# The weighted sum of the experts' second rows moves from VectorE to TensorE, in column tiles of 32

## The chip, the core and the metric

The kernel runs on one core of a Trainium2 chip. The metric is device time in microseconds (us) from start to end of one execution. The kernel before was run three times: 2932.58 us in the median (2925.65 to 2934.63).

## The reference, cut to what matters

Two transformer blocks follow each other on 512 tokens of width 1024, all in fp32. The first block has a state-space mixer and then a feed-forward of retrieved experts; the second has attention with pooling and then a gated feed-forward. The change touches the experts. For each token `xb`, 8 heads choose 16 of 16384 experts each, 128 in all. Every expert has a first row `u` and a second row `v` of 1024 numbers:

```
        i1 = jnp.take_along_axis(si[:, :, 0], ci // PEER_TOPK, axis=-1)
        i2 = jnp.take_along_axis(si[:, :, 1], ci % PEER_TOPK, axis=-1)
        eidx = i1 * PEER_N_KEYS + i2
        g = jax.nn.softmax(cs, axis=-1)
        u = expert_u[eidx]
        v = expert_v[eidx]
        act = jax.nn.gelu(jnp.einsum('td,thkd->thk', xb, u).astype(jnp.float32), approximate=False)
        return jnp.einsum('thk,thkd->td', (g * act).astype(v.dtype), v)
```

So 128 dot products with first rows give 128 weights, and the output is the sum of 128 second rows with these weights. The rows are read from memory: 512 tokens x 128 experts x 2 rows of 4 KB.

## The kernel before

The 512 tokens are four tiles of 128, with a token on each partition. The first block's mixer runs for tiles 0 and 1 (mixer 0) and then for tiles 2 and 3 (mixer 1), each followed by the choice of experts ("choose": queries and scores by TensorE, top-k by VectorE, then `slots`, `first` and `index`, which leave the expert numbers in `eidx`). The second block runs as attention of tiles 0 and 1, attention of tile 2, feed-forward of tiles 0 to 2, attention of tile 3, feed-forward of tile 3 (`SECOND`).

Beside this main stream runs the expert stream. Per tile it has 256 steps. In each, GpSimd issues one indirect DMA (L650), which gathers one row for each of the 128 tokens into one of eight buffers (`ring`, 128 x 1024): step k of the first half ("dots") takes the first row of every token's k-th expert, step k of the second half ("rows") takes the second row. VectorE works on each: the dots are multiply-and-sum against the token's own row `u2` (L1827), 128 columns of `dots`. Then ScalarE takes the gelu, VectorE multiplies by `gate` into `wgt`, and in the rows half each gathered tile is multiplied by a column of `wgt` and added to `acc` or `junke` in turn (L1833). `h3` adds the two to the token tile `h2`, and norms it; the second block may start on that tile only then. Gather number i waits until VectorE has done step i - 8, which frees its buffer.

Weights of the main stream come through three slots (`wr`), loaded by SyncE's queue. PSUM has eight banks: two rings of four, "lo" and "hi", from which each product takes the next bank, and waits until that bank's last reader is done.

The order on each engine is fixed when the program is built. `make_plan` merges the two streams by two clocks: the main stream's advances by its planned TensorE time or 1.5 times its planned VectorE time, whichever is more, times a pace for attention; the expert stream's by `EW[t]` (1.5, 1.6, 1.3, 2.0) a step. The stream that is behind goes next. Each engine then walks the same list of units and issues what it has in each, so an engine that waits in one unit holds back all later ones on it.

Of the kernel before, what the change touches and what calls it, by code (L numbers as in the profile page):

```python
# [7 lines left out]
U32 = mybir.dt.uint32  # L8
# [27 lines left out]
EW = (1.5, 1.6, 1.3, 2.0)  # L36
# [58 lines left out]
class Plan:  # L95
# [3 lines left out]
    def __init__(self):  # L99
        self.units, self.bank, self.slot, self.loads = [], {}, {}, []  # L100
        self.turn = {"lo": 0, "hi": 0}
        self.use = [None] * 8
        self.p = self.v = 0.0
# [6 lines left out]
    def take(self, key, which, emptied):  # L110

        i = self.turn[which] % 4 + (4 if which == "hi" else 0)
# [161 lines left out]
def plan_choose(pl, A, q, t0, t1, done):  # L274
# [12 lines left out]
    for hj in range(16):  # L287
# [6 lines left out]
        if hj % 2:  # L294
# [3 lines left out]
            yield True  # L298
    for t in range(t0, t1):
        pl.add("slots", q, t, v=2 * (vc(2048) + 0.2))  # L300
        pl.add("first", q, t, v=3 * vc(2048) + 1.0)
        yield True
        pl.add("index", q, t, v=vc(2048) + 0.4)
# [4 lines left out]
def plan_attend(pl, A, t0, t1):  # L308
# [31 lines left out]
    for u_ in range(len(units) + 2):  # L340
        for lag, part in enumerate(("front", "texp", "mixv")):
            if 0 <= u_ - lag < len(units):
# [5 lines left out]
                elif part == "texp":  # L348
                    while pl.turn["hi"] % 4 < 2:
                        pl.turn["hi"] += 1  # L350
                    pl.take(("texp", t, h), "hi", ("act", "texp", t, h))
                    pl.add("texp", t, h, p=0.12 * (t + 1))
                else:
                    if h == 0:
                        pl.hold(("mixv", t), 4 + t % 2, ("dve", "attn", t))
# [13 lines left out]
def plan_feed(pl, A, t0, t1):  # L369
# [12 lines left out]
    for hf in range(2):  # L382
        bs = list(range(nt)) if hf == 0 else list(range(4, 4 + nt))
        for t in range(nt):
            pl.hold(("down", t0, hf, t), bs[t], ("dve", "down", t0, hf, t))
# [67 lines left out]
def build(nc, A, out):  # L453
    with ExitStack() as ctx:
# [33 lines left out]
        junke = sb("junke", [128, 1024])  # L488
# [74 lines left out]
        with ExitStack() as pk:  # L563
            kT = sbx(pk, "kT", [128, 4, T])
# [46 lines left out]
        jobs = [u[1:] for u in pl.units if u[0] == "expert"]  # L611
        job_of = {u: i for i, u in enumerate(jobs)}
# [28 lines left out]
        def gpsimd(e):  # L641
            w = Waits(e)
            issued, chosen, base = 0, 0, 0

            def gather(k):
                t, which, j = jobs[k]
                w.wait_ge(*dve.at("index", t))
                if k >= NR:
                    w.wait_ge(*dve.at("expert", *jobs[k - NR]))
                e.indirect_dma_start(ring[k % NR][:], None, A[which],  # L650
                                     bass.IndirectOffsetOnAxis(ap=eidx[:, t, j:j + 1], axis=0)
                                     ).then_inc(gathered[k % NR], 16)
# [1303 lines left out]
```

## Time and profile before

| | |
|---|---|
| median of the runs | 2932.58 us |
| the profiled execution | 2928.44 us |
| its span | 2926.6 us |
| mean granted clock of TensorE | 0.826 of full |
| ScalarE busy | 638.5 us (22%) |
| GpSimd busy | 1261.4 us (43%) |
| read from memory | 793.75 MB |

The profile is of one execution, and its span runs from the first to the last instruction. Busy shares are means over stretches with different limits, so a table of stretches is read beside them. In the trace each fp32 matmul of the program is two records. `ring<-in_pu` are the gathers of first rows, `ring<-in_pv` those of second rows. All but a few of TensorE's matmuls go through one helper (L678), so they are told apart by their tiles and shapes.

### The profile page before, as it was taken

To read this page: it belongs to the slowest core of one execution; us is meant where nothing else is said; L and a number is where in the kernel's file an instruction comes from. 1 tells how busy PE (TensorE), PEld (TensorE's weight loads), DVE (VectorE), ACT (ScalarE), POOL (GpSimd) and SP (SyncE) were. 2 spreads that over 40 slices of the span, in tenths; PEclk is the share of its full clock that TensorE was granted. 3 is DMA by queue.
4 is the path that set the end of the run, shared out by engine and by line. 5 is a ranking of instruction groups with operands and counts; after the bars stand their busy time and mean duration, and the time that the engine had idled before them with its cause. 6 is when DMAs were issued, how large, how long until landed. Compare 5 with 4: busy or idle time off the path is not lost.

```text
span 2926.6 us, 26514 instructions
## 1 busy us (share of the span) xinstructions
PE 2019.9 (69%) x9256; PEld 1629.7 (56%) x9256; DVE 1854.2 (63%) x3630; ACT 638.5 (22%) x1713; POOL 1261.4 (43%) x1060
## 2 busy tenths in 40 slices
PE   7999989860887787796550031246348899993898
PEld 6888878750776676785440021234346555443685
DVE  2333310198688899867799978888976566754200
ACT  4555520110443433200210020011012200002210
POOL 0000000006576666566655656767755675641000
PEclk8999989985899888897875566665777999996899
DMA  4332324334799999899897579999987899984176
GB/s 165 110 128 108 115 94 146 109 141 171 259 353 368 347 361 370 330 414 382 316 378 266 183 278 411 358 362 335 387 321 282 322 381 390 406 322 172 63 253 245
DMA packets 178871, 797.62 MB, mean 273 GB/s; under 512 B 20001, under 2 KB 20257, under 8 KB 153137
## 3 DMA queue, kind: packets, MB, share of 16 engines
q0 software_dynamic: 147456, 536.94, 48.7%
q1 hardware_dynamic: 30704, 256.89, 23.1%
q10 hardware_dynamic: 576, 2.10, 0.2%
q8 instruction: 73, 1.20, 0.2%
q14 instruction: 62, 0.50, 0.0%
HBM read 793.75 MB, written 2.10 MB: 272 GB/s over the span
## 4 chain that ended last, share of the span: by engine, by line
PE 41%; DVE 23%; DMA 13%; issue 10%; POOL 7%; ACT 5%; DVEq 0%; ACTq 0%
PE ps L678 41%; DMA ring<-in_pu,eidx 9%; POOL ring L650 7%; DMA ring<-in_pv,eidx 3%; DVE acc L1833 3%; DVE junke L1833 3%; DVE junke L1827 2%; DVE acc L1827 1%; DVE si L1415 1%; DVE tmpx L1485 1%; DVE ci L1415 1%; DVE sv L1413 1%; DVE cv L1413 1%; ACT L1032 1%; ACT L1030 1%
## 5 line engine op out<-in xcount | busy, mean ns | idle before, releaser
L650 POOL DMA_INDIRECT ring<-in_pu,eidx x512 | 654.4, 1278 | 366.0 <-DVE dots L1827 221.3
L650 POOL DMA_INDIRECT ring<-in_pv,eidx x512 | 575.2, 1124 | 367.7 <-DVE acc L1833 121.5
L678 PE MATMUL ps<-uT,wr 128*128 128x256 f32 (+1 forms) x2304 | 533.6, 388 | 2.8 <-ACT ynT L1212 2.8
L678 PEld LDWEIGHTS ps<-uT,wr 128*128 128x128 f32 x2304 | 440.4, 193 | 72.1 <-issue 3.3
L678 PE MATMUL ps<-hT,wr 128*128 128x128 f32 (+2 forms) x1984 | 406.0, 369 | 8.7 <-ACT hT L1071 7.1
L678 PE MATMUL ps<-junk,h 128*128 128x128 f32 x256 | 49.5, 380 | 484.6 <-DVE junk L1436 484.6
L678 PEld LDWEIGHTS ps<-hT,wr 128*128 128x128 f32 x1984 | 304.1, 198 | 109.9 <-issue 8.1
L1827 DVE CUSTOM_DVE_ANT_0 junke<-ring,u 128x1024 f32<-128x1024 f32 x256 | 312.7, 1222 | 62.8 <-DMA ring<-in_pu,eidx 60.1
L1827 DVE CUSTOM_DVE_ANT_0 acc<-ring,u 128x1024 f32<-128x1024 f32 x256 | 313.0, 1222 | 43.2 <-DMA ring<-in_pu,eidx 40.3
L1833 DVE SCALAR_TENSOR_TENSOR acc<-ring,wgt,acc 128x1024 f32<-128x1024 f32 x252 | 324.9, 1289 | 12.1 <-DMA ring<-in_pv,eidx 12.0
L1833 DVE SCALAR_TENSOR_TENSOR junke<-ring,wgt,junke 128x1024 f32<-128x1024 f32 x252 | 325.0, 1290 | 8.3 <-DMA ring<-in_pv,eidx 8.2
L678 PEld LDWEIGHTS ps<-junk,h 128*128 128x128 f32 x256 | 47.6, 290 | 487.8 <-DVE junk L1436 487.8
L672 POOL TENSOR_TENSOR oh<-oh,sif 128x256 f32<-128x256 f32 x32 | 31.6, 1019 | 662.1 <-DVE oh L1631 662.0
L678 PE MATMUL ps<-wr,fT 128*128 128x512 f32 x352 | 151.5, 592 | 1.3 <-issue 1.3
L678 PE MATMUL ps<-wr,uT 128*128 128x256 f32 x512 | 124.6, 406 | 0.0
L678 PE MATMUL ps<-ynT,wr 128*128 128x256 f32 x512 | 115.8, 385 | 6.1 <-DVE g L1585 6.1
L678 PE MATMUL ps<-u2T,wr 128*128 128x256 f32 x512 | 117.6, 384 | 2.9 <-ACT u2T L1071 2.9
L1783 DVE TENSOR_TENSOR fT<-fT,ps 128x384 f32<-128x384 f32 (+1 forms) x44 | 18.5, 421 | 159.6 <-PE ps L678 159.6
L1485 DVE SCALAR_TENSOR_TENSOR tmpx<-xp,vec,tmpx 128x272 f32<-128x272 f32 (+1 forms) x128 | 63.1, 493 | 84.8 <-ACT tmpx L1104 82.5
L678 PEld LDWEIGHTS ps<-wr,uT 128*128 128x128 f32 x512 | 105.9, 208 | 17.1
L678 PEld LDWEIGHTS ps<-wr,fT 128*128 128x128 f32 x352 | 66.7, 190 | 85.2 <-issue 85.2
L678 PEld LDWEIGHTS ps<-ynT,wr 128*128 128x128 f32 x512 | 98.9, 194 | 20.7 <-issue 6.8
(260 smaller groups left out, 2502.5 us busy)
## 6 DMA issues: line engine op xcount, KB each, us to landing
wr<-in_wg SPq DMA_DIRECT2D x32, 1536.0 KB, 9.0
wr<-in_wgu SPq DMA_DIRECT2D x44, 1024.0 KB, 6.2
wr<-in_wsc SPq DMA_DIRECT2D x16, 1536.0 KB, 8.5
wr<-in_wso SPq DMA_DIRECT2D x16, 1536.0 KB, 8.2
wr<-in_wq SPq DMA_DIRECT2D x16, 1152.0 KB, 5.4
wr<-in_wqku SPq DMA_DIRECT2D x18, 1024.0 KB, 8.2
wr<-in_wdn SPq DMA_DIRECT2D x12, 1536.0 KB, 7.9
wr<-in_wgate SPq DMA_DIRECT2D x16, 1024.0 KB, 5.0
```

The costliest lines, as they stand in the source:

```text
L650: e.indirect_dma_start(ring[k % NR][:], None, A[which], bass.IndirectOffsetOnAxis(ap=eidx[:, t, j:j + 1], axis=0)).then_inc(gathered[k % N ...
L672: e.tensor_tensor(q4, q4, bmid(i4[:, h, 1, :], 16), MUL).then_inc(*pool.up("slots", q, t, h))
L678: return e.matmul(o, l, r, start=start, stop=stop, skip_group_check=True)
L1030: e.activation(a, v, ACT.Ln).then_inc(*act.up())
L1032: e.activation(a, a, ACT.Exp, scale=-0.5).then_inc(*act.up("root", *tag))
L1413: e.max(v8, x).then_inc(*dve.up())
L1415: e.max_index(i8, v8, x).then_inc(*dve.up())
L1485: e.scalar_tensor_tensor(out=tx[:] if k < 3 else xg[:, s_, :], in0=x[:, k:k + n], scalar=W["convw"][:, q4 + k:q4 + k + 1], in1=tx[:], op0= ...
L1783: e.tensor_tensor(fT[:, j, :], fT[:, j, :], b[:, 0:nr], MUL).then_inc(*dve.up("fT", t0, j))
L1827: e.tensor_tensor_reduce(two[:], row[:], u2[:], 1.0, 0.0, MUL, ADD, dots[:, k:k + 1]).then_inc(*dve.up(*u))
L1833: e.scalar_tensor_tensor(out=a_[:], in0=row[:], scalar=wgt[:, k:k + 1], in1=a_[:], op0=MUL, op1=ADD).then_inc(*dve.up(*u))
```

## The change

Second rows are now gathered by token: one indirect DMA takes the 128 rows of one token, one expert on each partition. For that the expert numbers are transposed by TensorE (unit `index`) and copied by ScalarE into `eidxT`, whose column t holds one token's experts. The weights `wgt` are transposed in the same way into `wT` (unit `wturn`). The sum over a token's experts is then a sum over partitions, which is a matmul: the stationary operand is a column of weights, the moving operand the gathered rows in two halves of 512 columns.

The output row must land on the token's own partition. The stationary operand is therefore a window of 32 columns of `wz`, which is zero but for every 32nd column; the window is placed so that the token's weights stand in column k. Its product adds the token's row to partition k of a quarter of the bank and zero to the other 31. The 128 tokens go in 32 units of four, one in each quarter (`32 * c`), and four matmuls for each half (`b[32 * c:32 * c + 32, :]`) are issued one behind another. Two banks, 6 and 7, hold the sums of a tile over its 32 units, and `h3` adds them to `h2`. `wz` is two buffers of 16 tokens' columns, filled by ScalarE from `wT`.

With it come: six PSUM banks in rings of three for the main stream, a single bank for attention's transposed exponentials, `kT` in the memory of the mixer's state `st`, and a step of 1.45 in the plan for dots and rows of all tiles. A dot now writes its product over the gathered rows. Gathers follow the plain numbering, 256 a tile.

```diff
-EW = (1.5, 1.6, 1.3, 2.0)
+DOT = 1.45
+ROW = 1.45
...
+    if q == 0:
+        pl.rings = {"lo": (0, 1, 2), "hi": (3, 4, 5)}
+        pl.turn = {"lo": 0, "hi": 0}
...
-                    while pl.turn["hi"] % 4 < 2:
-                        pl.turn["hi"] += 1
-                    pl.take(("texp", t, h), "hi", ("act", "texp", t, h))
+                    pl.hold(("texp", t, h), 5, ("act", "texp", t, h))
...
-        for which in ("pu", "pv"):
-            for k in range(128):
-                pl.add("expert", t, which, k, v=1.2)
-                if which == "pv" and k == 127:
-                    pl.add("h3", t, v=4 * vc(1024))
-                yield EW[t]
+        for k in range(128):
+            pl.add("dot", t, k, v=1.3)
+            yield DOT
+        pl.take(("wturn", t), "lo", ("act", "wturn", t))
+        pl.add("wturn", t)
+        for half in range(2):
+            pl.hold(("rows", t, half), 6 + half, ("dve", "h2e", t, half))
+        for k in range(32):
+            pl.add("rows", t, k)
+            if k == 31:
+                pl.add("h3", t, v=4 * vc(1024))
+            yield 4 * ROW
...
+                t, k = divmod(i, 256)
+                index, table, k = (eidx, "pu", k) if k < 128 else (eidxT, "pv", 32 * (k % 4) + (k - 128) // 4)
+                w.wait_ge(*act.at("index", t))
+                if i >= NR:
+                    t_, k_ = divmod(i - NR, 256)
+                    w.wait_ge(*(dve.at("dot", t_, k_) if k_ < 128 else pe.at("rows", t_, (k_ - 128) // 4)))
...
+                elif kind == "wturn":
+                    t = u[1]
+                    b = ps(*u)
+                    w.wait_ge(*dve.at("wgt", t))
+                    e.transpose(b[:, 0:128], wgt[:], ident).then_inc(*pe.up(*u))
+
+                elif kind == "rows":
+                    _, t, k = u
+                    w.wait_ge(*act.at("wz", t, k // 4))
+                    for c in range(4):
+                        i = 256 * t + 128 + 4 * k + c
+                        w.wait_ge(gathered[i % NR], 16 * (i // NR + 1))
+                    for half in range(2):
+                        b = ps("rows", t, half) if k == 0 else bank[6 + half]
+                        for c in range(4):
+                            i = 256 * t + 128 + 4 * k + c
+                            at = 31 + 32 * (4 * (k % 4) + c) - k
+                            x = mm(b[32 * c:32 * c + 32, :], wz[(k // 4) % 2][:, at:at + 32],
+                                   ring[i % NR][:, 512 * half:512 * half + 512], k == 0, k == 31)
                     x.then_inc(*pe.up(*u))
...
+                    e.activation(wgt[:], dots[:], ACT.Gelu).then_inc(*act.up("gelu", t))
+                    w.wait_ge(*pe.at("wturn", t))
+                    e.activation(wT[:], b[:, 0:128], ACT.Copy).then_inc(*act.up("wturn", t))
...
+                    if k % 4 == 0:
+                        r = k // 4
+                        for z in ((0, 1) if r == 0 else (r + 1,) if r < 7 else ()):
+                            w.wait_ge(*act.at("wturn", t))
+                            if t or z > 1:
+                                w.wait_ge(*pe.at("rows", *((t, 4 * z - 5) if z > 1 else (t - 1, 27 + 4 * z))))
+                            e.activation(wz[z % 2][:, 31:31 + 512:32].rearrange("p (k c) -> p k c", c=4),
+                                         wT[:].rearrange("p (c k) -> p k c", c=4)[:, 4 * z:4 * z + 4, :], ACT.Copy
+                                         ).then_inc(*act.up("wz", t, z))
...
-                    elif k < 2:
-                        e.tensor_scalar((acc, junke)[k][:], row[:], wgt[:, k:k + 1], None, MUL).then_inc(*dve.up(*u))
-                    else:
-                        a_ = (acc, junke)[k % 2]
-                        e.scalar_tensor_tensor(out=a_[:], in0=row[:], scalar=wgt[:, k:k + 1], in1=a_[:], op0=MUL,
-                                               op1=ADD).then_inc(*dve.up(*u))
-                    past.append(dve.n)
+                    e.tensor_tensor_reduce(row[:], row[:], u2[:], 1.0, 0.0, MUL, ADD, dots[:, k:k + 1]
+                                           ).then_inc(*dve.up(*u))
...
-                    e.tensor_tensor(acc[:], acc[:], junke[:], ADD).then_inc(*dve.up())
-                    then()
-                    e.tensor_tensor(h2[:, t, :], h2[:, t, :], acc[:], ADD).then_inc(*dve.up("h2e", t))
+                    for half in range(2):
+                        hv = h2[:, t, 512 * half:512 * half + 512]
+                        w.wait_ge(*pe.at("rows", t, 31))
+                        e.tensor_tensor(hv, hv, bank[6 + half][:], ADD).then_inc(*dve.up("h2e", t, half))
```

The order changes in three places that matter below. TensorE in mixer 1, in tile 0's rows half, before (`uT` and `wr`: products of the mixer; `xw`, `dD`, `xdt`, `mt`, `st`: its scan):

```order
L678 MATMUL ps<-wr,uT 128x256 x16
L678 MATMUL ps<-xw_1,btm_1 128x256
L678 MATMUL ps<-uT,wr 128x256 x8
L678 MATMUL ps<-dD_1,xc_1 128x128 x2
L678 MATMUL ps<-xdt_1,mt 128x64 x4
L678 MATMUL ps<-st,xc_1 128x256
L678 MATMUL ps<-uT,wr 128x256 x24
L774 MATMUL ps<-con,xc_1 128x128 x3
L678 MATMUL ps<-con,sla_1 128x128 x4
```

and now (`ring,wz`: the row matmuls, eight to a unit of four tokens):

```order
L691 MATMUL ps<-wr,uT 128x256 x16
L691 MATMUL ps<-ring,wz 32x512 x16
L691 MATMUL ps<-xw_1,btm_1 128x256
L691 MATMUL ps<-uT,wr 128x256 x8
L691 MATMUL ps<-dD_1,xc_1 128x128 x2
L691 MATMUL ps<-xdt_1,mt 128x64 x4
L691 MATMUL ps<-st,xc_1 128x256
L691 MATMUL ps<-uT,wr 128x256 x8
L691 MATMUL ps<-ring,wz 32x512 x8
```

The same mixer work has row units between its products, each of which waits for four gathers.

TensorE at the second block's feed-forward of tiles 0 to 2, before (`hT_0,wr`: gate and up products; `wr,fT`: down projection; `junk,h`: the norm of tile 3's attention):

```order
L678 MATMUL ps<-wr,mx 128x256 x32
L678 MATMUL ps<-junk,h 128x128 x24
L678 MATMUL ps<-hT_0,wr 128x384 x352
L678 MATMUL ps<-wr,fT 128x512 x132
L678 MATMUL ps<-junk,h 128x128 x8
```

and now:

```order
L691 MATMUL ps<-hT_0,wr 128x384 x8
L691 MATMUL ps<-ring,wz 32x512 x8
L691 MATMUL ps<-wr,fT 128x512 x6
L691 MATMUL ps<-ring,wz 32x512 x8
L691 MATMUL ps<-wr,fT 128x512 x9
L691 MATMUL ps<-ring,wz 32x512 x8
L691 MATMUL ps<-wr,fT 128x512 x117
L691 MATMUL ps<-junk,h 128x128 x8
```

The gate and up products are spread over the whole of tile 3's gathers, and 117 of the 132 down matmuls stand behind the last row unit.

VectorE about the `index` unit of tile 2, which lets its gathers begin, before (L1833: rows of tile 1; L1669 to L1675: the index; L1625: first of the slots of tile 3):

```order
L1833 SCALAR_TENSOR_TENSOR junke<-ring,wgt,junke 128x1024
L1833 SCALAR_TENSOR_TENSOR acc<-ring,wgt,acc 128x1024
L1669 TENSOR_REDUCE cx_1<-oh_1 128x128
L1672 SCALAR_TENSOR_TENSOR cx_1<-cx_1 128x128
L1675 CAST eidx<-cx_1 128x128
L1833 SCALAR_TENSOR_TENSOR junke<-ring,wgt,junke 128x1024
L1833 SCALAR_TENSOR_TENSOR acc<-ring,wgt,acc 128x1024
L1833 SCALAR_TENSOR_TENSOR junke<-ring,wgt,junke 128x1024
```

and now (L1902 to L1905: `h3` of tile 1; L1733 to L1741: the index):

```order
L1723 TENSOR_REDUCE cx_1<-oh_1 128x128
L1725 RECIPROCAL rd<-rd 128x8
L1727 TENSOR_TENSOR gate<-gate,rd 128x128
L1902 TENSOR_TENSOR h<-h,ps 128x512 x2
L1428 TENSOR_SCALAR se<-se 128x1
L1431 TENSOR_TENSOR se<-se 128x1
L1433 TENSOR_TENSOR se<-se 128x1
L1435 TENSOR_SCALAR se<-se 128x1
L1437 TENSOR_TENSOR se<-se 128x1
L1905 SCALAR_TENSOR_TENSOR h<-h,se,rowb 128x1024
L1733 TENSOR_REDUCE cx_1<-oh_1 128x128
L1738 SCALAR_TENSOR_TENSOR cx_1<-cx_1 128x128
```

Before, 33 row steps of tile 1 came behind this index; now the whole `h3` of tile 1 comes ahead of it.

## Rows read from the trace of the kernel before

**Rows 1.** The page: span, engine shares with instruction counts, and the gathers' queue

```profile
span 2926.6 us, 26514 instructions
...
PE 2019.9 (69%) x9256; PEld 1629.7 (56%) x9256; DVE 1854.2 (63%) x3630; ACT 638.5 (22%) x1713; POOL 1261.4 (43%) x1060
...
q0 software_dynamic: 147456, 536.94, 48.7%
```

**Rows 2.** Table of stretches (us from the span's start); its head names the columns

```profile
core 0: us, PE busy (x) PEld busy (x) DVE busy (x) ACT busy (x) POOL busy (x), PEclk, DMA share, GB/s
200.00:300.00 100.00, 100.00 (x505) 85.49 (x504) 36.15 (x91) 59.00 (x165) 0.00 (x0) 1.00 0.34 125
1200.00:1300.00 100.00, 100.00 (x465) 88.04 (x464) 68.06 (x113) 8.81 (x17) 62.13 (x50) 1.00 1.00 395
679.00:967.00 288.00, 189.54 (x888) 164.55 (x889) 227.38 (x449) 104.94 (x284) 189.12 (x143) 0.80 0.83 310
967.00:1206.00 239.00, 184.82 (x875) 161.22 (x874) 215.45 (x280) 96.79 (x284) 151.72 (x130) 0.86 0.92 351
1206.00:1467.00 261.00, 200.58 (x910) 174.93 (x909) 190.87 (x410) 26.77 (x62) 165.67 (x130) 0.88 0.95 369
1467.00:1718.00 251.00, 33.37 (x173) 29.58 (x171) 249.21 (x491) 9.21 (x22) 149.71 (x143) 0.57 0.78 290
1718.00:1933.00 215.00, 76.73 (x328) 65.83 (x328) 169.31 (x305) 20.96 (x46) 146.25 (x127) 0.67 0.91 347
1933.00:2137.00 204.00, 87.30 (x326) 68.70 (x326) 178.33 (x228) 25.77 (x72) 144.62 (x130) 0.60 0.95 363
2137.00:2286.00 149.00, 103.87 (x538) 90.11 (x538) 99.25 (x228) 37.98 (x99) 81.45 (x61) 0.74 0.79 293
2286.00:2628.00 342.00, 340.66 (x968) 183.76 (x968) 220.04 (x263) 15.39 (x28) 212.84 (x177) 1.00 0.95 370
```

**Rows 3.** Chain of waits: start us, us, what. The feed-forward of tiles 0 to 2

```profile
2286.58 227.28 PE ps L678 x704
2514.62 113.55 PE ps L678 x264
```

**Rows 4.** The page's costliest groups: gathers and VectorE's expert work

```profile
L650 POOL DMA_INDIRECT ring<-in_pu,eidx x512 | 654.4, 1278 | 366.0 <-DVE dots L1827 221.3
...
L650 POOL DMA_INDIRECT ring<-in_pv,eidx x512 | 575.2, 1124 | 367.7 <-DVE acc L1833 121.5
...
L1827 DVE CUSTOM_DVE_ANT_0 acc<-ring,u 128x1024 f32<-128x1024 f32 x256 | 313.0, 1222 | 43.2 <-DMA ring<-in_pu,eidx 40.3
L1833 DVE SCALAR_TENSOR_TENSOR acc<-ring,wgt,acc 128x1024 f32<-128x1024 f32 x252 | 324.9, 1289 | 12.1 <-DMA ring<-in_pv,eidx 12.0
```

**Rows 5.** Waits: engine line waited for: us in total, times, longest us

```profile
POOL ring L650 <- DVE dots L1827: 234.4, 80, 16.4
...
POOL ring L650 <- DVE acc L1833: 121.5, 36, 15.4
...
POOL ring L650 <- DVE junke L1833: 96.0, 33, 28.6
```

**Rows 6.** VectorE in order of time, h3 of tile 0: start us, us, what

```profile
1204.72 1.23 DVE L1840 TENSOR_TENSOR acc<-acc,junke 128x1024 f32<-128x1024 f32 x1
1205.98 1.22 DVE L1842 TENSOR_TENSOR h<-h,acc 128x1024 f32<-128x1024 f32 x1
...
1213.54 1.28 DVE L1812 SCALAR_TENSOR_TENSOR u<-h,rs,rowa 128x1024 f32<-128x1024 f32 x1
```

**Rows 7.** VectorE in order of time, from tile 0's index to its second dot

```profile
678.62 0.23 DVE L1675 CAST eidx<-cx 128x128 uint32<-128x128 f32 x1
...
684.47 1.23 DVE L1827 CUSTOM_DVE_ANT_0 junke<-ring,u 128x1024 f32<-128x1024 f32 x1 [4.22 <-DMA ring<-in_pu,eidx]
...
701.18 1.22 DVE L1827 CUSTOM_DVE_ANT_0 acc<-ring,u 128x1024 f32<-128x1024 f32 x1
```

**Rows 8.** TensorE in order of time: matmuls with 32 moving columns

```profile
22.93 7.98 PE L678 MATMUL ps<-wdt,uT 128*16 128x32 f32 x48 [0.95 <-ACT aneg L1080]
```

**Rows 9.** Chain of waits, end of the expert work

```profile
2637.72 2.71 DMA out<-hT
...
2667.41 1.15 ACT acc L1351 x2
...
2679.12 3.80 PE ps L678 x16
```

More of the change, by code:

```diff
@@ L110, in take @@
     def take(self, key, which, emptied):
-        i = self.turn[which] % 4 + (4 if which == "hi" else 0)
+        i = self.rings[which][self.turn[which] % len(self.rings[which])]
         self.turn[which] += 1
@@ L302, in plan_choose @@
         yield True
+        pl.take(("index", t), "lo", ("act", "index", t))
         pl.add("index", q, t, v=vc(2048) + 0.4)
@@ L487, in build @@
         u2 = sb("u2", [128, 1024])
-        junke = sb("junke", [128, 1024])
+        eidxT = sb("eidxT", [128, NT, 128], U32)
+        wT = sb("wT", [128, 128])
+        wz = [sb(f"wz{i}", [128, 16 * 32 + 32]) for i in range(2)]
         acc = sb("acc", [128, 1024])
@@ L642, in gpsimd, with gather @@
             w = Waits(e)
[L643 to L652, printed above, removed]
+            issued, chosen = 0, 0
+            def gather(i):
+                t, k = divmod(i, 256)
[4 more added lines that the diff above has]
+                    w.wait_ge(*(dve.at("dot", t_, k_) if k_ < 128 else pe.at("rows", t_, (k_ - 128) // 4)))
+                e.indirect_dma_start(ring[i % NR][:], None, A[table],
+                                     bass.IndirectOffsetOnAxis(ap=index[:, t, k:k + 1], axis=0)
+                                     ).then_inc(gathered[i % NR], 16)
             w.wait_ge(*pe.at("turn", ("mix", 0), 2))
             for u in pl.units:
-                if u[0] == "index":
-                    chosen = 256 * (u[2] + 1)
-                    while issued < min(chosen, NR):
-                        gather(issued)
-                        issued += 1
-                elif u[0] == "expert":
-                    k = job_of[u[1:]]
-                    while issued < min(chosen, k + NR + 1):
+                if u[0] in ("index", "dot", "rows"):
+                    if u[0] == "index":
+                        chosen, ahead = 256 * (u[2] + 1), NR
+                    elif u[0] == "dot":
+                        ahead = 256 * u[1] + u[2] + 1 + NR
+                    else:
+                        ahead = 256 * u[1] + 128 + 4 * u[2] + 4 + NR
+                    while issued < min(chosen, ahead):
                         gather(issued)
@@ L1432, in vector @@
                         e.memset(sm[:], 1.0).then_inc(*dve.up("smset"))
+                        for z in range(2):
+                            e.memset(wz[z][:], 0.0).then_inc(*dve.up("wzset"))
                     rsqrt(rs, sm[:, 0:k], sm[:, 16:16 + k], sm[:, 24:24 + k], 1.0 / 1024, tag)
@@ new lines, in vector @@
+                elif kind == "dot":
+                    _, t, k = u
+                    i = 256 * t + k
+                    row = ring[i % NR]
+                    if k == 0 and t:
+                        w.wait_ge(*act.at("gelu", t - 1))
+                    w.wait_ge(gathered[i % NR], 16 * (i // NR + 1))
+                    w.wait_ge(*dve.at("urow", t))
+                    e.tensor_tensor_reduce(row[:], row[:], u2[:], 1.0, 0.0, MUL, ADD, dots[:, k:k + 1]
+                                           ).then_inc(*dve.up(*u))
+                elif kind == "wturn":
+                    t = u[1]
+                    w.wait_ge(*act.at("gelu", t))
+                    e.tensor_tensor(wgt[:], wgt[:], gate[:, t, :], MUL).then_inc(*dve.up("wgt", t))
```

58 lines of the change are left out of this document (29 added, 29 removed).

## The prediction

> **What bounds the kernel now.** I read the page's header and engine shares first, then the table of stretches, then the costliest groups with the waits, then single rows. The profiled execution took 2928.4 us, a span of 2926.6 us and 1.8 us around it; the median of the runs is 2932.6 us, 4.2 us more, so I add 4 us at the end.
>
> No engine is full over the span: TensorE 69%, VectorE 63% [rows 1]. The gathers are 536.94 MB in 1024 transfers, 0.524 MB each [rows 1]. They run from 679 to 2664 us, and all of the change's sum lies there, so I cut that time at the ends of the two halves of each token tile (dots, then rows) [rows 2]. The reader is to see a different limit in each stretch:
> - Tile 0 rows (967 to 1206, 239 us): TensorE 185 us at a clock of 0.86, VectorE 215, DMA share 0.92. All three near full.
> - Tile 1 rows (1467 to 1718, 251 us): VectorE 249, TensorE 33, DMA 0.78. VectorE alone bounds it.
> - Tile 2 rows (1933 to 2137, 204 us): DMA 0.95, VectorE 178, TensorE 87 at clock 0.60.
> - Feed-forward of tiles 0 to 2 (2286 to 2628, 342 us): TensorE 341, DMA 0.95. TensorE runs 704 and then 264 records with no gap [rows 3]. This is where tile 3 has its rows half.
>
> DMA share 1.00 stood at 395 GB/s [rows 2]; over the full stretches 370 GB/s stood at 0.95, which is 389. I take 390 GB/s as what the gathers can reach. So DMA has little to give: 5 to 8% in three of the four rows halves. Only tile 1 has a large reserve.
>
> **What goes and what comes.** VectorE loses 504 multiply-adds of 1289 ns [rows 4], 650 us, and 8 cheaper first products; two adds of 1.23 and 1.22 us per tile [rows 6] become two of half the width. The dots stay as they are, 1222 ns each [rows 4], and so does each gather in size. The waits of GpSimd for a free buffer, 234 us on dots and 217 us on the sums [rows 5], show that VectorE was late in both halves; in the rows halves this now turns on TensorE. GpSimd itself needs 1.12 to 1.28 us a gather [rows 4], less than any step takes.
>
> TensorE gains 1024 matmuls of 512 columns, 256 a tile, each with 32 output rows. The feed-forward's down projection has the same moving shape: 264 records (two to a matmul) in 113.55 us [rows 3], 0.430 us a record, 0.860 us a matmul. That is the price if column tiles do not overlap. No row here has column tiles side by side, so the price c of a matmul is the unknown. From above: 0.860. From below: four at once, 0.215. A row for small operands, 48 records in 7.98 us, 0.166 us a record [rows 8], says that each record may have a floor, which would lift the lower end to 0.33 if it held for 32-column weights. I take 0.430, for this reason: each fp32 matmul is two records on one tile, the second cannot stream until the first has, and the matmuls are issued in order; so the second record of one tile can overlap only with the first of the next. A pair is then half hidden.
>
> The Trainium skill, "TensorE: Matmul & The Clock Gate", Part 3, gives 2.38 times for three column tiles of 512 columns, and says that matmuls start and end in program order. The second statement is what my half rests on; the first, scaled as an estimate to four tiles, would be about 0.27 us a matmul and by the sum below a result near 2945. No run here has shown either yet. "TensorEngine Tiling (Array Packing)", Key Properties, adds a rule against this change: a switch of tiling mode drains the engine.
>
> **Stretch by stretch**, from rows 2, with c in us:
> 1. Tile 0, rows half. TensorE has 875 records of the mixer. Mixer 0 ran 505 records in 100 us at clock 1.0 and no gap [rows 2], so they need 173 us, less some 5% since mixer 1 has 256 columns for 272: 165 us. With the new work 165 + 256c, against 239 before. DMA's floor is 351 GB/s x 239 us / 390 = 215 us. At c = 0.43 it is 275, +36 us.
> 2. Tile 1, rows half. VectorE keeps 249 - 165 = 84 us and no longer bounds. DMA: 290 x 251 / 390 = 187 us. TensorE: 33 us, about 42 more of choose products that the new order puts here, plus 110, is 185. Both near full with TensorE waiting for four rows at a time, so I take 196. But the new order puts the index of tile 2 behind the h3 of tile 1, where it stood 33 multiply-adds ahead. No gather can be issued while h3 runs (1204.72 to 1214 us in tile 0, 10 us [rows 6]), then index and its transposition some 6 us, and after nine gathers GpSimd waits for the slots of tile 3. At tile 0 the same pattern gave the index at 678.62, the first dot at 684.47 and the second at 701.18 [rows 7], so some 12 us more. Together 28 us. 196 + 28 - 251 = -27 us.
> 3. Tile 2. Slots and index of tile 3, some 18 us of VectorE (15 between the two dots, 3 at the index [rows 7]), moves into a dots half of 215 us with 46 us idle: +8. Rows half: 87 + 110 = 197 of TensorE, DMA floor 363 x 204 / 390 = 190: -5. Sum +3.
> 4. Tile 3 up to the feed-forward: 76 gathers in place of 56 beside attention. DMA 43.7 + 10.5 MB at 390 is 139 us, under the 149; VectorE gets 20 dots, 23 us, beside 99: +5 us.
> 5. Feed-forward of tiles 0 to 2. The gate and up products are spread over all gathers and 117 of the 132 down matmuls come behind the last row. Nothing of TensorE's is hidden: 341 + 256c. Attention of tile 3 follows it after the norm, as after h3 before, 12 us from 2667 to 2679 [rows 9]. Before, 2286 to 2679 was 393 us. At c = 0.43: 341 + 110 + 12 - 393 = +70 us.
> 6. Tiling switches, two to each of 128 row units: 0 to 0.2 us each, bounded above by one small record; half of them where TensorE bounds: 0.05 us x 128, +7 us. The three transpositions and copies by ScalarE per tile (the gelu chain, 1 us of it there before) sit behind prefetched rows: nothing, at worst 5 us a tile. PSUM rings of three banks for four: nothing, since ScalarE, which empties most of them, was busy 97 of 239 us [rows 2]; at worst 20 us in mixer 1, where TensorE would wait for a bank.
>
> The end, 2679 to 2926, has no gathers and keeps its 247 us.
>
> Where TensorE bounds two stretches the sum is 512c - 74 (the 239 less 165) - 40 - 27 + 3 + 5 + 7 = 512c - 126 us. At c = 0.430: +94. 2928.4 + 94 = 3022, and 4 us to the median: **3026 us**. It is even at c = 0.246.
>
> **The rivals.**
> - *Column tiles do not overlap* (c = 0.86). For it: no row shows overlap, fp32 takes two records. Against: the tokens alternate between four tiles, so neighbours are free of each other. Then tile 1 is TensorE-bound too (75 + 220 + 28 for 224: +99) and tile 2 (87 at half clock, 60 at full, + 220 for 199: +81). 512 x 0.86 - 126 + 180 = +494: 3425 us.
> - *Four at once* (c = 0.215 to 0.27): 512c - 126 = -16 to +12, 2917 to 2945 us: no change, since DMA takes over in tile 0 (its floor 215 against TensorE's 220) and the down projection still stands alone.
> - *Faster*: at c up to 0.23, the freed VectorE also lets the mixer's convolutions go ahead of the products, and the gathers reach 390 GB/s in all rows halves. Tile 0 215 (-24), tile 1 187 + 16 (-48, with half of the stall hidden behind attention's products), tile 2 -14, feed-forward 341 + 55 + 8 - 393 = +11. Sum -75 + 5: about 2862 us. For it: VectorE's 249 of 251 us in tile 1. Against: DMA at 0.92 to 0.95 elsewhere. It decides from c = 0.23.
> - The gather of one token's 128 rows costs the same as 128 tokens' one row: both are 128 packets of 4 KB at random. That it would not is given no case of its own.
>
> **How the numbers follow.** Half overlap 0.47 (own range 2975 to 3100: c between 0.40 and 0.50, item 6, and a clock of 0.60 as in tile 2, at which its new work could cost up to 40 us more); no overlap 0.19; four at once without gain 0.17; faster 0.17. A measurement tells about 0.3%, 9 us. Half overlap gives faster in 0.03 and same in 0.03 of the whole; four at once is spread over the three, 0.05, 0.06, 0.06. So faster 0.25, same 0.09, slower 0.66. The range 2862 to 3290 takes in both good cases and a partial overlap, and leaves out the serial one.
>
> **What would show it.** The row matmuls' start-to-start in the new profile: 0.43 us says half, 0.22 four at once, 0.86 none. TensorE with no gap over the feed-forward at about 450 us; the last gather ahead of the down projection, which runs 101 us with an idle DMA; the tile 1 rows half at 196 us and a hole of some 28 us in the gathers behind it. If the row matmuls are at 0.43 and the mixer's second half is still 239 us, item 1 is wrong, and its 165 us was too high.

## The result, and the profile after

The changed kernel took 3078.15 us in the median of four runs (3075.79 to 3080.02), the kernel before 2929.47 us beside it: a ratio of 1.0507, 95% interval 1.0488 to 1.0526. It is slower by 5%, as forecast in sign; the forecast was 3026 us. But the mechanism that I gave the most weight is not the one that the trace shows, as the experiments below tell.

The page of the changed kernel: span, engine shares, and the groups of the expert work. It answers to [rows 1, 4].

```profile
span 3074.8 us, 29657 instructions
...
PE 2320.8 (75%) x11312; PEld 1674.6 (54%) x11312; DVE 1229.9 (40%) x3120; ACT 646.9 (21%) x1752; POOL 1177.8 (38%) x1060
...
L663 POOL DMA_INDIRECT ring<-in_pu,eidx x512 | 657.5, 1284 | 346.5 <-DVE dots L1889 165.1
L663 POOL DMA_INDIRECT ring<-in_pv,eidxT x512 | 492.3, 962 | 500.6 <-PE ps L691 365.4
L1889 DVE CUSTOM_DVE_ANT_0 ring<-ring,u 128x1024 f32<-128x1024 f32 x512 | 608.1, 1223 | 139.4 <-DMA ring<-in_pu,eidx 134.7
...
L691 PE MATMUL ps<-ring,wz 128*32 128x512 f32 x2048 | 307.8, 728 | 172.6 <-DMA ring<-in_pv,eidxT 171.3
```

VectorE's share fell from 63% to 40%, 624 us less, and the kernel is slower all the same. TensorE gained 301 us of busy time. The last row is the one to read: 2048 records of row matmuls are 307.8 us of TensorE, 0.30 us a matmul with whatever stands between, where one record alone is said to last 728 ns in the mean. They overlap.

The table of stretches of the changed kernel, cut at the same events as [rows 2]: gelu and h3 of each tile, then the down projection and the end.

```profile
core 0: us, PE busy (x) PEld busy (x) DVE busy (x) ACT busy (x) POOL busy (x), PEclk, DMA share, GB/s
676.00:962.00 286.00, 185.97 (x846) 159.59 (x846) 224.48 (x444) 100.50 (x278) 190.13 (x144) 0.79 0.84 310
962.00:1230.00 268.00, 236.19 (x1364) 158.17 (x1365) 67.32 (x158) 98.85 (x286) 117.79 (x125) 0.94 0.86 317
1230.00:1484.00 254.00, 194.38 (x859) 167.02 (x857) 170.04 (x304) 28.28 (x66) 167.19 (x132) 0.90 0.95 372
1484.00:1713.00 229.00, 149.03 (x801) 69.50 (x801) 87.73 (x439) 14.54 (x42) 119.81 (x128) 0.78 0.86 315
1713.00:1945.00 232.00, 62.44 (x254) 52.10 (x250) 189.07 (x333) 21.36 (x47) 168.39 (x139) 0.65 0.86 319
1945.00:2191.00 246.00, 169.14 (x919) 85.95 (x919) 19.43 (x94) 24.37 (x76) 121.72 (x130) 0.80 0.83 300
2191.00:2453.00 262.00, 184.81 (x765) 139.15 (x762) 180.24 (x369) 48.26 (x114) 170.57 (x133) 0.76 0.89 336
2453.00:2698.00 245.00, 236.59 (x1024) 109.41 (x1024) 9.08 (x17) 10.82 (x26) 113.29 (x121) 0.98 0.91 339
2698.00:2824.00 126.00, 100.66 (x238) 44.34 (x234) 12.47 (x27) 14.87 (x23) 0.00 (x0) 0.91 0.27 96
2824.00:3075.00 251.00, 215.26 (x1340) 180.23 (x1340) 31.91 (x121) 41.15 (x103) 0.00 (x0) 0.89 0.51 180
```

Set beside the kernel before, with the halves cut at each gelu and at the first addition to `h2` of each h3 in both traces (us, to within 1; the row of "before, new order" and the others are experiments, below):

| | to 1st | dots 0 | rows 0 | dots 1 | rows 1 | dots 2 | rows 2 | dots 3 | rows 3 | end | span |
|---|---|---|---|---|---|---|---|---|---|---|---|
| before | 679 | 287 | 240 | 255 | 256 | 216 | 197 | 285 | 251 | 261 | 2926.6 |
| changed | 677 | 286 | 267 | 254 | 230 | 232 | 246 | 262 | 246 | 377 | 3074.8 |
| changed, old step | 679 | 288 | 274 | 260 | 242 | 213 | 236 | 287 | 304 | 263 | 3046.0 |
| before, new order | 679 | 286 | 240 | 253 | 252 | 237 | 208 | 259 | 208 | 376 | 2998.2 |
| changed, ten buffers | 677 | 279 | 241 | 246 | 210 | 226 | 215 | 249 | 242 | 370 | 2952.5 |
| ten buffers, old step | 677 | 282 | 255 | 252 | 209 | 215 | 220 | 285 | 296 | 262 | 2951.4 |
| changed, in pairs | 677 | 289 | 259 | 255 | 216 | 240 | 225 | 262 | 242 | 377 | 3041.1 |

The 148 us are therefore: rows half of tile 0 +27, of tile 1 -27, tile 2 +16 and +48, tile 3 with all behind it +87. The reader is to see two things. In the rows halves of tiles 0 and 2 the DMA share fell (0.92 to 0.86, and 0.95 to 0.83) though VectorE was now busy for only 67 of 268 and 19 of 246 us there; in tile 1, where VectorE had been the bound, it rose (0.78 to 0.86). And 126 us stand behind the last row unit, in 101 of which TensorE makes down products at a DMA share of 0.27.

### The profile page after: what moved, and what is told of

Read it like the earlier page. It is cut to its first block, busy times and chain, and to the rows that moved or that the text cites. A ratio compares the mean times of both kernels' runs of the same rounds, so it can differ in the third digit from the quotient of the medians.

```text
span 3074.8 us, 29657 instructions
## 1 busy us (share of the span) xinstructions
PE 2320.8 (75%) x11312; PEld 1674.6 (54%) x11312; DVE 1229.9 (40%) x3120; ACT 646.9 (21%) x1752; POOL 1177.8 (38%) x1060
## 4 chain that ended last, share of the span: by engine, by line
PE 46%; DMA 21%; DVE 13%; POOL 11%; ACT 5%; issue 5%; DVEq 0%; ACTq 0%
PE ps L691 45%; POOL ring L663 11%; DMA ring<-in_pv,eidxT 11%; DMA ring<-in_pu,eidx 9%; DVE ring L1889 4%; ACT L1073 1%; ACT L1071 1%; ACT junk L1097 1%; DVE oh L1719 1%; DVE si L1477 1%; DVE tmpx L1549 0%; DVE sv L1475 0%; DVE ci L1477 0%; DMA out<-hT 0%; DVE cv L1475 0%
## 5 line engine op out<-in xcount | busy, mean ns | idle before, releaser
L663 POOL DMA_INDIRECT ring<-in_pv,eidxT x512 | 492.3, 962 | 500.6 <-PE ps L691 365.4
L1889 DVE CUSTOM_DVE_ANT_0 ring<-ring,u 128x1024 f32<-128x1024 f32 x512 | 608.1, 1223 | 139.4 <-DMA ring<-in_pu,eidx 134.7
L691 PE MATMUL ps<-uT,wr 128*128 128x256 f32 (+1 forms) x2304 | 540.7, 391 | 7.4 <-DVE scT L1583 4.0
L691 PE MATMUL ps<-ring,wz 128*32 128x512 f32 x2048 | 307.8, 728 | 172.6 <-DMA ring<-in_pv,eidxT 171.3
L691 PE MATMUL ps<-hT,wr 128*128 128x128 f32 (+2 forms) x1984 | 415.7, 372 | 9.0 <-ACT hT L1112 7.2
L691 PEld LDWEIGHTS ps<-ring,wz 128*32 128x32 f32 x2048 | 65.9, 123 | 341.4 <-issue 334.8
L691 PE MATMUL ps<-wr,uT 128*128 128x256 f32 x512 | 116.4, 387 | 0.0
L691 PEld LDWEIGHTS ps<-u2T,wr 128*128 128x128 f32 x512 | 96.2, 193 | 26.1 <-issue 14.0
L691 PE MATMUL ps<-up,wpl 128*128 128x128 f32 (+1 forms) x24 | 10.2, 523 | 128.9 <-DVE up L1778 128.9
L691 PEld LDWEIGHTS ps<-wr,uT 128*128 128x128 f32 x512 | 99.2, 195 | 14.9 <-issue 0.8
```

The lines of the kernel that those rows point to most:

```text
L663: e.indirect_dma_start(ring[i % NR][:], None, A[table], bass.IndirectOffsetOnAxis(ap=index[:, t, k:k + 1], axis=0)).then_inc(gathered[i % ...
L691: return e.matmul(o, l, r, start=start, stop=stop, skip_group_check=True)
L1889: e.tensor_tensor_reduce(row[:], row[:], u2[:], 1.0, 0.0, MUL, ADD, dots[:, k:k + 1]).then_inc(*dve.up(*u))
```

## The experiments

**What a row matmul costs.** In the changed kernel a unit of eight matmuls, 16 records, and what follows it (TensorE in order of time: start us, us, what):

```profile
2633.28 1.92 PE L691 MATMUL ps<-ring,wz 128*32 128x512 f32 x16
2635.14 1.24 PE L691 MATMUL ps<-hT,wr 128*128 128x384 f32 x3
```

From start to start 1.86 us for eight: 0.232 us a matmul. Experiment e4 puts all four tokens of a unit on one column tile:

```diff
-                            x = mm(b[32 * c:32 * c + 32, :], wz[(k // 4) % 2][:, at:at + 32],
+                            x = mm(b[0:32, :], wz[(k // 4) % 2][:, at:at + 32],
```

> The changed kernel with the four matmuls of a unit half all on column tile 0 (the sums of the other three quarters are left out and tile 0's is a mixture). If the overlap seen in the changed kernel (8 matmuls from 2633.28 to 2635.14 us, 0.232 us each) comes from the four column tiles, a matmul takes 0.86 us now, and a unit 6.9 us; the kernel takes about 3450 us. If two records of one tile could overlap (an overlap that has nothing to do with the tiles), it stays at 0.23 and at 3078 us.

It took 3557.7 us (one run). The same view:

```profile
3000.71 7.05 PE L691 MATMUL ps<-ring,wz 128*32 128x512 f32 x16
3007.70 5.43 PE L691 MATMUL ps<-hT,wr 128*128 128x384 f32 x16
```

6.99 us for eight, 0.874 us each, the price of [rows 3]. The overlap is that of four column tiles, 3.8-fold, and it goes when the tiles are one. Each rows half grew, tile 0 to 406 us and tile 3 to 404. Without overlap the kernel is 480 us slower than the changed one, 108 us above what I expected of e4, and some 626 slower than the kernel before; my rival of that name had 494. The loss in the ring of buffers (below) was in none of my sums, which is probably the difference.

**Whether TensorE's work lengthens the rows halves.** Experiment e2 leaves out the second half's matmuls in 30 of 32 units:

```diff
-                    for half in range(2):
+                    for half in range(2 if k in (0, 31) else 1):
```

> The changed kernel without the row matmuls of the second 512 columns (but for the first and last unit of a tile), so half of the row work of TensorE, 30 us a tile, is gone; the rest of the output's columns is left out. Theory 'ring': the rows halves are paced by eight buffers that come free four at a time (a burst of four issues of 1.24 us, 6.4 us to landing, then the wait for TensorE), so tile 2's rows half stays at 235 to 246 us and tile 0's at 255 to 268. Rival 'TensorE work': they shorten by the work taken out, to about 216 and 238 us.

3023.6 us (one run). The rows halves were 257, 216, 234 and 227 us: shorter by 10, 14, 12 and 18 for 28 us of work taken out. Between the theories: a third to two thirds of the work is in the time, and tile 2 keeps 36 of its 48 us. So TensorE's work is a part of the loss and not all of it.

**The ring of buffers.** What GpSimd waits for in the changed kernel, and TensorE (us in total, times, longest):

```profile
POOL ring L663 <- PE ps L691: 391.5, 112, 13.4
...
PE ps L691 <- DMA ring<-in_pv,eidxT: 171.3, 59, 8.2
```

And the cause, GpSimd and TensorE in order of time:

```profile
2542.45 0.94 POOL L663 DMA_INDIRECT ring<-in_pv,eidxT  x1 [3.35 <-PE ps L691]
2543.69 0.94 POOL L663 DMA_INDIRECT ring<-in_pv,eidxT  x1 [0.30 <-issue]
2544.93 0.94 POOL L663 DMA_INDIRECT ring<-in_pv,eidxT  x1 [0.30 <-issue]
2546.18 0.94 POOL L663 DMA_INDIRECT ring<-in_pv,eidxT  x1 [0.30 <-issue]
...
2555.52 1.92 PE L691 MATMUL ps<-ring,wz 128*32 128x512 f32 x16 [0.79 <-DMA ring<-in_pv,eidxT]
```

A unit ends, and four buffers come free at once. GpSimd needs 1.24 us for each of the four issues, so the last one starts 3.7 us later and lands 6.4 us after that (the median of the page for these gathers); then the unit waits until TensorE is through a product of the feed-forward (5.4 us). Here the last of the four was issued at 2546.18, and the unit that needs it began at 2555.52, after TensorE had stood 0.79 us for it. With eight buffers only two units are under way. (3.7 + 6.4 + 1.9) / 2 is 6 us a unit without that wait, and measured are 245 / 32 = 7.7. Before, VectorE freed one buffer every 1.3 us. Experiment e3 has ten buffers:

```diff
-NR = 8
+NR = 10
...
-        acc = sb("acc", [128, 1024])
...
+                    if q:
+                        ring.append(sbx(pb, "ring9", [128, 1024]))
...
-                    e.activation(acc[:], h2[:, t, :], ACT.Square, accum_out=se[:, 0:1]
+                    e.activation(u2[:], h2[:, t, :], ACT.Square, accum_out=se[:, 0:1]
```

> The changed kernel with ten row buffers for eight, all else alike. Theory 'ring': the rows halves shorten by up to a fifth where DMA is under 0.90: tile 2 from 246 to about 210, tile 0 from 268 to about 250, tile 1 from 229 to about 205 us; in all 60 to 90 us less, 2990 to 3020 us. Rival 'TensorE work' or 'DMA is full': under 20 us less, 3060 or more.

2955.7 us, a ratio of 1.0083 (1.0067 to 1.0100) to the kernel before: 122 us less than the changed kernel, more than I had expected. The rows halves of tiles 0 to 3 in its table of stretches, and GpSimd's wait for TensorE:

```profile
955.00:1195.00 240.00, 226.25 (x1355) 154.64 (x1359) 67.23 (x157) 98.38 (x286) 117.19 (x124) 0.97 0.94 358
1441.00:1651.00 210.00, 140.54 (x801) 70.02 (x801) 91.31 (x438) 15.53 (x43) 119.82 (x126) 0.83 0.90 338
1877.00:2092.00 215.00, 161.09 (x919) 82.23 (x919) 19.59 (x94) 24.34 (x76) 123.01 (x131) 0.83 0.93 351
2340.00:2583.00 243.00, 236.05 (x1024) 108.78 (x1025) 10.03 (x20) 11.11 (x27) 112.69 (x121) 0.98 0.93 348
```

```profile
POOL ring L664 <- PE ps L692: 305.6, 104, 13.6
```

DMA share is 0.90 to 0.94, where the changed kernel had 0.83 to 0.91, and tiles 0 to 2 need 241, 210 and 215 us. By the table the four rows halves gained 81 of the 122 us. The dots halves, in which VectorE frees one buffer at a time in both kernels, gained 34 (6 to 13 each), so not all of the gain is the mending of the units of four.

The same run answers a rival that I gave no case: that gathers by token are dearer for the DMA engines than gathers by expert. Its queue of gathers:

```profile
q0 software_dynamic: 147456, 536.94, 48.2%
```

48.2% of 2952.5 us is 1423 us; before it was 48.7% of 2926.6 us, 1425 us, for as many packets and bytes [rows 1]. They cost the same.

Experiment e6 keeps eight buffers and frees them in twos:

```diff
-                    for c in range(4):
-                        i = 256 * t + 128 + 4 * k + c
-                        w.wait_ge(gathered[i % NR], 16 * (i // NR + 1))
...
+                    for pair in range(2):
+                        for c in (2 * pair, 2 * pair + 1):
+                            i = 256 * t + 128 + 4 * k + c
+                            w.wait_ge(gathered[i % NR], 16 * (i // NR + 1))
...
+                        x.then_inc(*(pe.up(*u) if pair else pe.up("pair", t, k)))
```

> The changed kernel with its row units cut in two: TensorE waits for two gathers, makes their four matmuls (two column tiles side by side, two halves), and frees two buffers, then the other two. Eight buffers as before. Only two tiles can overlap, so a matmul should take about 0.43 us for 0.232 and TensorE's row work rise from 60 to 110 us a tile. Theory 'burst': freeing two at a time is worth more than that where TensorE has room: rows halves of tiles 1 and 2 fall by 10 to 25 us, those of tiles 0 and 3 rise by up to 30, in all 3050 to 3090 us. Rival 'TensorE work': every rows half rises by a third to all of the 50 us, 3150 us or more.

3044.2 us: a ratio of 1.0347 (1.0298 to 1.0395), where the changed kernel had 1.0507. TensorE in order of time, four matmuls and the next product:

```profile
2108.47 1.91 PE L691 MATMUL ps<-ring,wz 128*32 128x512 f32 x8 [1.44 <-DMA ring<-in_pv,eidxT]
2110.32 3.72 PE L691 MATMUL ps<-wr,mx 128*128 128x256 f32 x16
```

1.85 us for four, 0.46 us each, where a pair stands alone. Where the second pair has landed as well, both run together, and a unit takes what it takes in the changed kernel, 1.87 us for eight:

```profile
2585.53 1.94 PE L691 MATMUL ps<-ring,wz 128*32 128x512 f32 x16
2587.40 2.85 PE L691 MATMUL ps<-hT,wr 128*128 128x384 f32 x8
```

So TensorE's row work did not rise from 60 to 110 us a tile, as I had expected. By the page it rose by 42 us in all four tiles, from 307.8, and TensorE's wait for gathers fell from 171.3 us:

```profile
L691 PE MATMUL ps<-ring,wz 128*32 128x512 f32 x2048 | 349.6, 644 | 84.6 <-DMA ring<-in_pv,eidxT 72.9
```

TensorE had more row work and not less, and still the rows halves of tiles 0 to 3 fell by 8, 14, 21 and 4 us, where I had expected tiles 0 and 3 to rise. What speaks for speed in this edit is only the smaller step: TensorE begins with two rows in place of four, and frees two buffers in place of four, the first two earlier. These two go together in e6, and no run parts them. The time lies in the step in which the ring is used up and freed.

Is it a gain for any kernel of this kind? Experiment e7 gives the kernel before nine buffers, with `kT` laid into `st` as in the changed one:

```diff
-NR = 8
+NR = 9
...
-            kT = sbx(pk, "kT", [128, 4, T])
+            kT = st[:].rearrange("p a b -> p (a b)").rearrange("p (a b) -> p a b", a=4)
```

> The kernel before with nine row buffers for eight (kT laid into the mixer's state to make room). If more buffers help any kernel that lives from these gathers, it gains some 20 to 40 us (2890 to 2910), half of what two more gave in the changed kernel at most. If they only mend the burst of four that the changed kernel made, it stays within 10 us of 2931.

A ratio of 0.9938 (0.9919 to 0.9957), some 16 us, between my two expectations. VectorE, which frees singly, is helped a little by one buffer; the unit of four was helped by 4%, with two buffers.

**The order.** Experiment e1 gives the changed kernel the old step of the plan, which puts the down products back beside the gathers and the index of tile 2 ahead of h3:

```diff
-DOT = 1.45
-ROW = 1.45
+EW = (1.5, 1.6, 1.3, 2.0)
```

> The changed kernel with the plan's step per tile of the kernel before (1.5, 1.6, 1.3, 2.0) for dots and rows in place of 1.45 throughout. Theory 'cover': the changed plan put 117 of 132 down products of the first feed-forward behind the last gather, where they run alone (TensorE 101 of 126 us, DMA share 0.27); with 2.0 for tile 3 they come back beside the gathers. Then the stretch behind h3 of tile 3 falls from 377 to some 265 us, tile 3's rows half grows by 20 to 40, and the kernel takes 2975 to 3010 us. Rival 'TensorE is full there': the row work has merely displaced the products and the time stays within 15 us of 3078, since tile 3's rows half grows by as much as the end falls.

3048.5 us, 1.0390 (1.0367 to 1.0412): 30 us less, not 70 to 100. The end fell by 114 us, but tile 3 took 84 of it. Its two stretches from h3 of tile 2 to gelu 3 and from gelu 3 to h3 of tile 3 (first column the stretch, then its length, then TensorE, weight loads, VectorE, ScalarE, GpSimd, clock, DMA share, GB/s):

```profile
2192.00:2480.00 288.00, 235.05 (x941) 167.95 (x938) 180.79 (x374) 51.24 (x120) 177.57 (x132) 0.85 0.88 327
2480.00:2784.00 304.00, 282.53 (x1084) 120.22 (x1082) 14.84 (x26) 14.89 (x32) 113.97 (x122) 0.97 0.83 295
```

TensorE is the bound in the second (283 of 304 us), as item 5 said. Experiment e5 is the other half of the cross: the kernel before, with VectorE's sums, in the new order.

```diff
-EW = (1.5, 1.6, 1.3, 2.0)
+EW = (1.45, 1.45, 1.45, 1.45)
```

> The kernel before with only the plan's step set to 1.45 for all tiles, so that VectorE still makes the sums but the order of the two streams is that of the changed kernel (down products of the first feed-forward behind the last gather, index of tile 2 behind h3 of tile 1). Theory 'plan': this order alone costs what the old step gave back in the changed kernel, some 30 us, in the end stretch (260 to 370 us) less what tile 3's halves win (about 80): 2950 to 2985 us. Rival 'the order only hurts where TensorE also has the rows': the kernel before has room on TensorE, and it stays within 10 us of 2931.

2999.0 us, 1.0190 (1.0141 to 1.0238), more than either of my expectations: the order alone costs 1.1% (the changed kernel over e1, 1.0507 / 1.0390) to 1.9% (e5), and the move to TensorE 3.1% (the changed kernel over e5) to 3.9% (e1) of its own. e5 and the changed kernel have the same order and differ in who makes the sums, which makes tile 3's rows half the cleanest comparison. In e5, that half and what is behind it:

```profile
2416.00:2624.00 208.00, 164.10 (x483) 93.22 (x482) 168.76 (x145) 8.22 (x17) 137.37 (x121) 0.89 0.99 398
2624.00:2740.00 116.00, 99.92 (x233) 43.89 (x231) 10.43 (x20) 9.93 (x16) 0.00 (x0) 0.94 0.26 92
```

208 us at a DMA share of 0.99, against 245 us at 0.91 with TensorE's units of four. By the table of halves e5 is faster in rows 0, 2 and 3 (27, 37 and 38 us) and slower in rows 1 (22 us), where VectorE also chooses; the rest is alike.

Experiment e8 has both, ten buffers and the old step:

> The changed kernel with ten row buffers and the plan's step per tile of the kernel before. If the two losses are separate their gains add: 3048 - 122 = 2926 us, and between 2910 and 2935; tile 3's rows half stays TensorE-bound near 300 us. If the ring's gain was mostly in stretches that the plan changes, less: 2950.

2949.4 us, 1.0027 (1.0006 to 1.0048). They do not add: with ten buffers the step is worth 0.6%, since tile 3 is bound by TensorE (296 us) whatever the ring.

**The banks.** Experiment e11 is the kernel before with only the PSUM layout of the change:

```diff
+    if q == 0:
+        pl.rings = {"lo": (0, 1, 2), "hi": (3, 4, 5)}
+        pl.turn = {"lo": 0, "hi": 0}
...
-                    pl.take(("texp", t, h), "hi", ("act", "texp", t, h))
+                    pl.hold(("texp", t, h), 5, ("act", "texp", t, h))
...
```

> The kernel before with only the changed kernel's PSUM layout: rings of three banks for four, one bank for attention's transposed exponentials, down projection in banks 0 to 5 (banks 6 and 7 stay unused). I had put this at nothing, at worst 20 us in mixer 1: within 10 us of the kernel before. Rival 'banks': it costs 20 us or more, in the halves beside mixer 1, and then it is part of what the changed kernel lost in tile 0.

1.0009 (0.9986 to 1.0032): nothing, as priced.

**A better version.** Experiment e9: ten buffers, tiles 0 to 2 on TensorE with the step 1.45, tile 3 on VectorE with the step 2.0. The sums of tile 3 use `rowa` and the space of `wz`, which are free by then.

```diff
+        if t == NT - 1:
+            pl.add("wturn", t)
+            for k in range(128):
+                pl.add("sum", t, k, v=1.3)
...
+                    else:
+                        w.wait_ge(*dve.at("sum", t, k - 2))
+                        e.scalar_tensor_tensor(out=a_, in0=row[:], scalar=wgt[:, k:k + 1], in1=a_, op0=MUL,
+                                               op1=ADD).then_inc(*dve.up(*u))
```

> Ten row buffers; tiles 0 to 2 make their sums on TensorE as in the changed kernel with the plan's step 1.45, tile 3 makes them on VectorE as the kernel before, with the step 2.0 for it, since there the feed-forward fills TensorE. If the stretches add: 2092 us to h3 of tile 2 (as with ten buffers), then about 796 us (as before): 2885 to 2900 us, 1 to 1.5% below the kernel before. If instead the two ways disturb each other (VectorE's sums lag at the change-over, or the gathers of tile 3 gain nothing), 2910 to 2930 us.

2918.7 us, a ratio of 0.9931 (0.9905 to 0.9957): the fastest of all, with e10 below and the kernel before on nine buffers (0.9938), from which it cannot be told apart. It is above the 2885 to 2900 us of stretches that add, and in the range of my rival, that the two ways disturb each other. Up to h3 of tile 2 it took 2108 us for 2092 in e3; dots and rows of tile 2 were 16 and 21 us behind the kernel before, rows of tile 1 47 ahead. Tile 3 with all behind it, on VectorE again, took 812 us for 796.

Experiment e10, the same with units cut in two:

> The same with the row units of tiles 0 to 2 cut in two, two buffers freed at a time. With ten buffers the burst is mended for the most part already: theory 'burst' says within 10 us of the mixed kernel, either way, since 50 us more of TensorE work a tile stand against finer release; tile 0's rows half, where TensorE is near full, gets longer by 5 to 15 us. A gain over 15 us would say that the burst still ruled.

2918.8 us, 0.9927 (0.9902 to 0.9952): no difference, as the theory said for ten buffers.

## Why the prediction was right or wrong

The sign and the range held, and the number was 52 us low. That is luck: the term that made the sum positive was wrong by 101 us (512 x (0.430 - 0.232)), and losses that stood in no term took its place.

- *The price c.* The step that failed first is "the second record of one tile can overlap only with the first of the next". It gave 0.430 us; measured are 0.232 (changed kernel), 0.46 for a pair alone on two tiles (e6), 0.874 with one (e4). So the price falls with the number of tiles, and the two records of an fp32 matmul do not halve the overlap. The floor of 0.166 us a record from [rows 8] did not hold either: 16 records in 1.86 us are 0.116 each. By the Trainium skill, "TensorE: Matmul & The Clock Gate", Part 3, the estimate was 0.27, nearer; this case's 3.8-fold over four tiles is above its 2.38-fold over three in proportion. The statement there that matmuls start and end in program order, on which my half rested, does not agree with e6: started in that order, the second pair could begin only once the first pair had begun its second matmul on the same tiles, 0.86 us in, and needs 1.85 us itself, so a unit would take 2.7 us, and 1.87 are measured. Of the drain at a switch of tiling mode (the Trainium skill, "TensorEngine Tiling (Array Packing)", Key Properties) no run here gives the price alone. The 1.86 us from a unit's start to the next product hold one switch, so it is small beside what e4 adds.
- *The sum with the right c* would have been 512 x 0.232 - 126 = -7 us, no change: my rival "four at once". It measured +148. So the mechanism that made the kernel slow was in none of my cases.
- *Item 1*, tile 0: 165 + 59 = 224 us by the sum, 267 measured. What was missing is for the most part the ring. I had written "TensorE waiting for four rows at a time" in item 2 and added 9 us for it in one tile; that the buffers come free in fours with it stood in no term. Ten buffers (e3) take 27 of the 43 us off this half, freeing in twos (e6) 8; with ten TensorE is busy for 226 of 240 us, so 224 was near its work, and the other 16 are time in which it stands.
- *Item 2*, tile 1: put at -27 us and measured at -27, but not for the reason given. I had 196 us for the rows half and 28 for the stall behind it. The rows half alone took 230 us, and 210 with ten buffers, so it has a loss of the ring too. The stall is there, but most of it falls behind h3, in the dots half of tile 2. The first gather of tile 2 starts 20 us after the last one of tile 1 (1704.91):

```profile
1724.78 1.06 POOL L663 DMA_INDIRECT ring<-in_pu,eidx  x1 [13.41 <-ACT eidxT L1385]
```

VectorE's 249 of 251 us was the one bound that the change removed; that reading held.
- *Item 3*, tile 2: +8 for the dots half, measured +16; with the old step it was 213, and 237 in e5, so it is the order, in which the index moved and with it that stall. Its rows half was put at -5 and was +48, the largest miss: 31 us of it go with ten buffers.
- *Item 4*: put at +5 us. From h3 of tile 2 to the first gate product it was 2131 to 2286.6 before, and 2191 to 2370.8 now: +24 us. The same stretch took 178 us in e5 (2154.9 to 2332.4), which has the new order and VectorE's sums, and 172 in e3. So it is mostly the order, with 76 gathers beside attention in place of 56; I had priced those 20 gathers by bytes, and their dots as hidden beside VectorE's 99 us. The stretch before and now:

```profile
2130.00:2287.00 157.00, 104.29 (x540) 90.44 (x541) 102.14 (x236) 43.08 (x106) 83.35 (x62) 0.73 0.80 297
2191.00:2371.00 180.00, 112.49 (x542) 96.87 (x540) 124.46 (x275) 42.73 (x106) 112.69 (x85) 0.67 0.85 317
```

VectorE is busy 22 us longer, about what the stretch gained, and no engine is full. That the dots stand in the way of attention's own work on VectorE would fit; no run tries it.
- *Item 5*: "nothing of TensorE's is hidden" was right, and is the one loss that stays with ten buffers. By rows of the changed kernel:

```profile
2370.84 72.48 PE L691 MATMUL ps<-hT,wr 128*128 128x384 f32 x224 [1.75 <-ACT hT L1112]
```

```profile
2697.97 100.69 PE L691 MATMUL ps<-wr,fT 128*128 128x512 f32 x234
2824.40 3.78 PE L691 MATMUL ps<-junk,h 128*128 128x128 f32 x16 [25.74 <-DVE junk L1500]
```

From 2370.8 to 2798.7 are 428 us for 341 + 59 = 400 of work, and the norm chain took 26 us for the 12 that I put, probably since VectorE and ScalarE still have the outputs of tiles 0 to 2 ahead of it (not tried). Measured 454 against 392 before, +61, where the sum with the right c has 341 + 59 + 12 - 393 = +19: 28 us in which TensorE stands between its work and 14 of the norm chain are what it lacks.
- *Item 6*: the banks cost nothing (e11); the switches were not measured alone.
- *The order* was in the sum only as a place where nothing is hidden. e5 shows that it has a price of its own, 1.9% without any row on TensorE: after its last gather there are 100 us of down products at a DMA share of 0.26.

What stays open is the cause of item 4's size, what is left of tile 2's loss with ten buffers, and why the old step brings so little in tile 0 (e1's and e8's rows 0 are 7 and 15 us above their twins with 1.45).

## What to carry to other kernels

When the consumer of a ring of buffers is exchanged, price how it frees them, not only how long it works: freed four at once, a ring of eight fed the DMA engines so unevenly that two more buffers gave back 4%, two thirds of it in the halves that freed in fours, while the 624 us saved on VectorE gave nothing outside tile 1. A stretch in which one engine has every microsecond taken (TensorE in the feed-forward) is best left alone even if the new work there is four times cheaper than feared. And where a plan's step is set anew with a change, cross the two: old engine with new order and new engine with old order cost two runs, and they split the loss.

## What the runs showed of the hardware

Four fp32 matmuls of 32 output rows and 512 moving columns, on four column tiles and issued one behind another, take 0.93 us together; on one tile 3.50. A tile does not wait for the others: in e6 the matmuls of a second pair of tiles, issued behind all those of the first pair, run beside them, eight in 1.87 us. The duration that the profile gives to one record says nothing of this. Row matmuls of the changed kernel and of e4 (ns min/median/max):

```profile
L691 PEld LDWEIGHTS ps<-ring,wz x2048: 105/110/178, 964.2 to 2697.0; 128*32 128x32 f32 x187
L691 PE MATMUL ps<-ring,wz x2048: 589/592/1065, 964.2 to 2697.4; 128*32 128x512 f32 x187
```

```profile
L691 PE MATMUL ps<-ring,wz x2048: 589/592/1063, 963.2 to 3182.5; 128*32 128x512 f32 x187
```

The medians are the same 592 ns; only starts, or the group's busy time over its count, tell the price. And the load of 32 columns took 110 ns in the median where that of 128 columns took 192 (1984 loads of the feed-forward's `hT`), so weights for narrow tiles did not hold the overlap back.
